# Scan products of a state-space block, two state tiles at a time on parts of the TensorE array

## The reference, cut to what matters

```python
ug = u.reshape(bsz, L, 64, 16)                      # 64 groups of 16 channels, L = 256
bu = einsum('gpc,blgc->blgp', b_bar, ug)            # complex, 64 states a group
h  = scan of h = lam_bar * h + bu along the tokens
y  = einsum('gcp,blgp->blgc', c, h).real + d_skip * ug
```

## Time and profile before

| what | value |
|---|---|
| median of three executions | 2492.57 us |
| profiled execution, its own time | 2492.02 us |
| its span, first to last instruction | 2490.4 us |
| mean granted TensorE clock | 0.964 of full speed |
| TensorE matmuls busy | 2356.1 us, 95% |
| VectorE busy | 1641.5 us, 66% |
| ScalarE busy | 978.7 us, 39% |
| GpSimd busy | 366.8 us, 15% |
| convolution stage with the scan | from 124.2 us to about 654 us |

### The profile page before, as it was taken

The page is one execution under the profiler, slowest core; times in us unless marked ns, Lnnn a source line. Parts: engine busy times, 40 slices in busy tenths (PEclk is TensorE's granted clock), DMA queues, the critical chain, the costliest instruction groups (busy, mean ns, idle before and its releaser), DMA issues.

```text
span 2490.4 us, 52181 instructions
## 1 busy us (share of the span) xinstructions
PE 2356.1 (95%) x20536; PEld 2260.4 (91%) x20536; DVE 1641.5 (66%) x2055; ACT 978.7 (39%) x1210; POOL 366.8 (15%) x214
## 2 busy tenths in 40 slices
PE   5999999999999999699997799899999999999997
PEld 5999999999999999699995677689999999999997
DVE  7688888888545677666798544277565656554444
ACT  4433333333444444433444211244434343434443
POOL 3265555554200000200002000000000000000000
PEclk9999999999999999899997877799999999999999
DMA  5544444445555655255553000035555555555553
GB/s 203 194 162 154 162 163 170 167 160 185 178 185 186 211 174 186 97 185 187 180 194 98 2 2 2 18 125 183 191 185 185 185 185 186 185 171 187 186 185 131
DMA packets 107710, 390.69 MB, mean 157 GB/s; under 512 B 12016, under 2 KB 12144, under 8 KB 107376
## 3 DMA queue, kind: packets, MB, share of 16 engines
q1 hardware_dynamic: 104544, 377.34, 45.8%
q0 software_dynamic: 2656, 11.01, 1.3%
q10 hardware_dynamic: 432, 1.21, 0.1%
HBM read 387.42 MB, written 2.10 MB: 156 GB/s over the span
## 4 chain that ended last, share of the span: by engine, by line
PE 77%; DVE 16%; issue 4%; ACT 1%; DVEq 0%; DMA 0%; ACTq 0%
PE ps_main L1499 22%; PE ps_main L1501 22%; PE ps_main L1500 21%; DVE w_lo L853 5%; PE ps_main L1710 2%; PE ps_aux L1710 1%; PE ps_main L1834 1%; PE ps_main L1833 1%; PE ps_aux L1800 1%; PE ps_aux L1799 1%; PE ps_aux L1499 1%; ACT w_hi L503 1%; DVE m L990 1%; DVE m L991 1%; PE ps_aux L1501 1%
## 5 line engine op out<-in xcount | busy, mean ns | idle before, releaser
L853 DVE TENSOR_TENSOR w_lo<-w_raw,w_hi 128x1024 fp32r<-128x1024 f32 x718 | 943.2, 1328 | 505.2 <-ACT w_hi L503 495.8
L503 ACT ACTIVATE w_hi<-w_raw 128x1024 fp32r<-128x1024 f32 x718 | 749.6, 1047 | 829.6 <-PE ps_main L1501 745.5
L1499 PE MATMUL ps_main<-xs,w_hi 128*128 128x256 f32 x1520 | 430.1, 283 | 10.1 <-DVE w_lo L853 10.1
L1501 PE MATMUL ps_main<-xs,w_lo 128*128 128x256 f32 x1520 | 424.9, 280 | 0.0
L1500 PE MATMUL ps_main<-xs,w_hi 128*128 128x256 f32 x1520 | 424.1, 279 | 0.0
L1499 PE MATMUL ps_main<-x3s,w_hi 128*128 128x256 f32 x1408 | 394.4, 280 | 0.0
L1501 PE MATMUL ps_main<-x3s,w_lo 128*128 128x256 f32 x1408 | 392.8, 279 | 0.0
L1500 PE MATMUL ps_main<-x3s,w_hi 128*128 128x256 f32 x1408 | 392.8, 279 | 0.0
L1499 PEld LDWEIGHTS ps_main<-xs,w_hi 128*128 128x128 f32 x1520 | 284.7, 187 | 18.5 <-DVE w_lo L853 11.5
L1500 PEld LDWEIGHTS ps_main<-xs,w_hi 128*128 128x128 f32 x1520 | 285.3, 188 | 0.4
L1501 PEld LDWEIGHTS ps_main<-xs,w_lo 128*128 128x128 f32 x1520 | 285.4, 188 | 0.0
(11 more groups left out here) (390 smaller groups left out, 4301.4 us busy)
## 6 DMA issues: line engine op xcount, KB each, us to landing
w_raw<-wmain SPq DMA_DIRECT2D x622, 512.0 KB, 3.3
w_raw<-wdown SPq DMA_DIRECT2D x80, 512.0 KB, 3.6
b_stage<-bst POOLq DMA_DIRECT2D x8, 512.0 KB, 5.2
w_raw<-wdown SPq DMA_DIRECT2D x16, 256.0 KB, 2.7
bias<-bias POOLq DMA_DIRECT2D x8, 384.0 KB, 3.3
x_res<-xt POOLq DMA_DIRECT2D x4, 512.0 KB, 7.2
out<-x_res SPq DMA_DIRECT2D x4, 512.0 KB, 2.7
x_res<-xt SPq DMA_DIRECT2D x2, 512.0 KB, 5.9
```

What stands on the lines that cost most here:

```text
L503: nc.scalar.activation(whi[:, s, 0:width], raw[:, s, 0:width], ACT.Copy).then_inc(hi_ready, 1)
L853: V.tensor_tensor(wlo[:, s, 0:width], raw[:, s, 0:width], whi[:, s, 0:width].bitcast(F32), ALU.subtract)\
L1499: nc.tensor.matmul(out, whi[:, s, w], xs_[:, 0, k, :], start=(first and kk == 0), stop=False)
L1501: ins = nc.tensor.matmul(out, wlo[:, s, w], xs_[:, 0, k, :], start=False, stop=(last and kk == kbs - 1))
```

## The change

`b_stage` no longer holds the stored zeros: the 32 rows of each state tile stand on that tile's own 32 partitions, and a matmul of `scan_bu` takes 32 rows of the array (`tile_position=(32 * t, 0)`) with all 128 columns. The load of `b_stage` shrinks from 512 KB to 128 KB a block. The tokens' operand comes from a fixed copy, `u_stage`, that ScalarE makes once a block (`stage_u`): ahead of the loop after `trig(0)`, and in a block at p = 9 after `trig(i + 1)`. TensorE waits for that copy (`u_staged`) before the first products of a block.

`scan_bu` and `scan_y` handle a pair of tiles in one go, in the order part 0 of both tiles, then part 1 of both. The input products stay at p = 0 and 3; the output products go from p = 4, 5, 8, 9 to p = 5 and 9. Each output product still has 128 rows and 32 columns.

```diff
-        bstage = wk("b_stage", 96, [TPB, 2, P])
+        bstage, ustage = wk("b_stage", 96, [2, P]), wk("u_stage", 97, [L])
...
-        SCAN_BU, SCAN_IN, SCAN_Y = (0, 0, 3, 3), (0, 1, 4, 5), (4, 5, 8, 9)
+        SCAN_BU, SCAN_IN, SCAN_Y = (0, 3), (0, 1, 4, 5), (5, 9)
...
                     if p == 9 and not last:
                         trig(i + 1)
+                        act.wait_ge(bu_ready, i * TPB + TPB)
+                        stage_u(i + 1)
...
+            def stage_u(i):
+                nc.scalar.activation(ustage[:, :], slot(ug, i) if not isinstance(i, int) else ug[:, i, :], ACT.Copy)\
+                    .then_inc(u_staged, 1)
+
             trig(0)
+            stage_u(0)
             with act.Fori(0, SB - 1) as i:
...
-            def scan_bu(i, t):
-
-                if t == 0:
+            def scan_bu(i, pair):
+
+                t0 = 2 * pair
+                if pair == 0:
                     pe.wait_ge(b_loaded, i * 16 + 16)
-
-                pe.wait_ge(bu_used, (i * TPB if t < 2 else i * TPB + (t - 1)) + GO)
-                uj = ug[:, bass.ds(i, 1), :].rearrange("p a n -> p (a n)")
-                nc.tensor.matmul(aux[:, t % 2, 0:L], bstage[:, t, 0, :], uj, start=True, stop=True)
-                nc.tensor.matmul(aux[:, t % 2, L:2 * L], bstage[:, t, 1, :], uj, start=True, stop=True)\
-                    .then_inc(bu_ready, 1)
+                    pe.wait_ge(u_staged, i + 1)
+                pe.wait_ge(bu_used, i * TPB + t0 + GO)
+                for part in range(2):
+                    for t in (t0, t0 + 1):
+                        rows = slice(32 * t, 32 * t + 32)
+                        ins = nc.tensor.matmul(aux[:, t % 2, part * L:(part + 1) * L], bstage[rows, part, :], ustage[rows, :],
+                                               start=True, stop=True, tile_position=(32 * t, 0))
+                        if part == 1:
+                            ins.then_inc(bu_ready, 1)
...
-                pe.wait_ge(h_ready, i * TPB + (t + 1) + GO)
-                out = aux[32 * t:32 * t + 32, 2, 0:L]
-                nc.tensor.matmul(out, cstage[:, t, 0, :], hs[:, t % 2, 0, :], start=True, stop=False,
-                                 tile_position=(0, 32 * t))
-                nc.tensor.matmul(out, cstage[:, t, 1, :], hs[:, t % 2, 1, :], start=False, stop=True,
-                                 tile_position=(0, 32 * t)).then_inc(h_used, 1)
+                pe.wait_ge(h_ready, i * TPB + (t0 + 2) + GO)
+                for part in range(2):
+                    for t in (t0, t0 + 1):
+                        ins = nc.tensor.matmul(aux[32 * t:32 * t + 32, 2, 0:L], cstage[:, t, part, :], hs[:, t % 2, part, :],
+                                               start=(part == 0), stop=(part == 1), tile_position=(0, 32 * t))
+                        if part == 1:
+                            ins.then_inc(h_used, 1)
...
-                    for t in range(TPB):
-                        if SCAN_BU[t] == p:
-                            scan_bu(i, t)
-                        if SCAN_Y[t] == p:
-                            scan_y(i, t)
+                    if p in SCAN_BU:
+                        scan_bu(i, SCAN_BU.index(p))
+                    if p in SCAN_Y:
+                        scan_y(i, SCAN_Y.index(p))
```

More of the change, by code:

```diff
@@ L263, in hybrid_kernel @@
         xg_ready, xn_ready, xhi_ready, xs_ready = sem("xg_ready"), sem("xn_ready"), sem("xhi_ready"), sem("xs_ready")
-        ones_ready, c_prime, ga_copied, ga_sig = sem("ones_ready"), sem("c_prime"), sem("ga_copied"), sem("ga_sig")
+        u_staged, ones_ready, c_prime, ga_copied, ga_sig = sem("u_staged"), sem("ones_ready"), sem("c_prime"), sem("ga_copied"), sem("ga_sig")
         ybh_ready, f_ready, mh_ready, x_again = sem("ybh_ready"), sem("f_ready"), sem("mh_ready"), sem("x_again")
@@ L392, in scan_b @@
                 src = bst_dram[0] if isinstance(i, int) else bst_dram[bass.ds(i, 1)].rearrange("a p n -> p (a n)")
-                pool.dma_start(bstage[:, :, :, :], src).then_inc(b_loaded, 16)
+                pool.dma_start(bstage[:, :, :].rearrange("p a n -> p (a n)"), src).then_inc(b_loaded, 16)
             def scan_c(i):
@@ L1558, in scan_y @@
-            def scan_y(i, t):
-                if t == 0:
+                    pe.wait_ge(u_staged, i + 1)
[7 more added lines that the diff above has]
+                            ins.then_inc(bu_ready, 1)
@@ L1561, in scan_y @@
+            def scan_y(i, pair):
+                t0 = 2 * pair
+                if pair == 0:
                     pe.wait_ge(c_staged, i + 1)
                     pe.wait_ge(y_used, i + GO)
-                pe.wait_ge(h_ready, i * TPB + (t + 1) + GO)
-                out = aux[32 * t:32 * t + 32, 2, 0:L]
-                nc.tensor.matmul(out, cstage[:, t, 0, :], hs[:, t % 2, 0, :], start=True, stop=False,
-                                 tile_position=(0, 32 * t))
-                nc.tensor.matmul(out, cstage[:, t, 1, :], hs[:, t % 2, 1, :], start=False, stop=True,
-                                 tile_position=(0, 32 * t)).then_inc(h_used, 1)
+                pe.wait_ge(h_ready, i * TPB + (t0 + 2) + GO)
[5 more added lines that the diff above has]
+                            ins.then_inc(h_used, 1)
@@ L2003, in _layout @@
     arrays["xt"] = np.ascontiguousarray(f["x"][0].T.reshape(KB, P, L).transpose(1, 0, 2))
-    bst = np.zeros((SB, P, TPB, 2, P), np.float32)
+    bst = np.zeros((SB, P, 2, P), np.float32)
     cs = np.zeros((P, 2, STATE_TILES, 32), np.float32)
@@ L2008, in _layout @@
         for g in range(64):
-            j, t, h = g // 8, g % 8 // 2, g % 2
-            bst[j, (g % 8) * 16:(g % 8) * 16 + 16, t, r, h * 64:h * 64 + 64] = b[g].T
+            j, h = g // 8, g % 2
+            bst[j, (g % 8) * 16:(g % 8) * 16 + 16, r, h * 64:h * 64 + 64] = b[g].T
             cs[h * 64:h * 64 + 64, r, g // 2, h * 16:h * 16 + 16] = c[g].T
-    arrays["bst"] = bst.reshape(SB, P, TPB * 2 * P)
+    arrays["bst"] = bst.reshape(SB, P, 2 * P)
     arrays["cs"] = cs
```

## The result

The changed kernel takes 2510.78 us (median of eight executions; the kernel before 2492.47 in eight), a ratio of 1.0062 with a 95% interval of 1.0043 to 1.0082. By the ratio it is slower by some 15 us, by the two medians by 18. The forecast was 2495.4, "no change", with a range of 2485 to 2510: the median lies just above its upper end, and the ratio times the median before (2508) just inside it.

A forecast was written before the change was run, and what follows sets the result against it. VectorE's w_lo chain paces each block up to unit 15, PE the rest. First block +3.39, crossings +0.5, last block gaining 2.84, clock +1.7: +2.8 on 2492.02, 2494.8; with 0.55 for the median 2495.4 us, range 2485 to 2510.

The forecast's parts named there:

- Block split into A and B: A, end of unit 0 to unit 15's w_lo, VectorE paces; B, to the next unit 0's end, PE paces, savings count.
- Input pair, 1.27 us: scan_bu pair on PE: 1.27 instead of 1.85 us, 0.58 saved, 0.48 where PE comes straight from dense work.
- Output pair, 1.18 us saved: scan_y pair on PE: two tiles side by side take 1.18 instead of 2.36 us.
- Wait for `u_stage`: PE before each block's first products: waits 1.8 us, 3.9 in the first block; blocks stay at 66.5 us.
- Last block: No w_lo to wait for, so it gains 0.48 + 2 x 1.18 = 2.84 us.
- The clock: One half-clock stretch, 1.7 us, behind the first block's wait; none added for gaps in the seven blocks.
- the sum of +2.8: Whole kernel against the profiled 2492.02 us: net +1.1 from the blocks, 1.7 for the clock, giving 2494.8.
- the clock falls in every block: Rival: half-clock stretch behind unit 15's gap, 1.7 us in each of seven blocks, 12 us, 2507; chance 0.12.
- the two slower rivals: Tiles do not run side by side, 2509 us, chance 0.10; clock falls in every block, 2507, chance 0.12.

The follow-up runs named there:

- The pair with tripled output products: Kernel of the early copy with one pair's output products issued three times, at p = 5 or at p = 9; ratios 0.9956 and 0.9998.
- the plain wait: Kernel before with only the copied operand, u_stage made behind trig and PE's wait for it, products as before; ratio 1.0078.
- the kernel with the output products alone: Kernel before with the changed kernel's scan_y, output products in pairs at p = 5 and 9; ratio 0.9961.
- the kernel of the early copy: Changed kernel with u_stage made early: in the zb stage for the first block, at p = 6 for the others; ratio 0.9953.
- The kernel with the filled gap: Changed kernel with fifteen dense matmuls on TensorE ahead of its wait for u_stage in each block; ratio 1.0022.

## Why the prediction came out as it did, step by step

- **Block split into A and B**: right. Savings in A went into the waits for `w_lo` (10.1 us in 7 before, 19.8 in 14 after, at units 11 and 15). The pair with tripled output products shows it from the other side.
- **Input pair, 1.27 us**: right. Its eight passes take 1.13 us from first start to last end, and with them a block is 0.57 to 0.67 shorter than with the plain wait (67.80 against 68.37 to 68.47, all without a half-clock stretch), where 0.58 was forecast. Row tiles of 32 rows run side by side as those of 64 did.
- **Output pair, 1.18 us saved**: right, 1.15 by the kernel with the output products alone.
- **Wait for `u_stage`**: right in place, with gaps of 1.78 us and 3.93 in the first block, 1.8 and 3.9 forecast. A block without a half-clock stretch is 66.6 us, not 66.48: the copy takes 0.40 us, not the 0.36 read off `gate_a`, and PE starts 0.13 behind it, not 0.05. Over seven crossings that is about 1 us.
- **Last block**: right. From its first input products to the gb stage it was forecast 3.42 shorter (2.84, and the 0.58 that I had counted with the crossing); it is 1.83 shorter (62.87 against 64.70) with a half-clock stretch that cost some 1.5 in it, and 3.37 shorter in the kernel of the early copy, which has none.
- **The clock**: this is the step that failed. "In the seven blocks the gaps become about 1.7 us at `stage_u` and 1.9 at unit 15 ... I add none." The term for the clock was put at one stretch, 1.7 us. All eight gaps at `stage_u` were followed by a half-clock stretch, each worth 1.5 to 1.6 us: 12.3 us instead of 1.7. With it and the 1 us above, the sum of +2.8 becomes +14.4, against 14.7 measured for the stage. The rival "the clock falls in every block" had the right size, and 0.12 of the chance; it had the place wrong, at unit 15's stall, where the changed kernel has none and other kernels three in all. I compared gaps by length alone (1.45 kept, 2.19 fell). The kernel with the filled gap shows that the idle time is needed; the early copy, that the light products without it are harmless. Why the gaps of 1.78 us fell here and not in the kernel with the wait alone stays open: lighter work behind them and another place in time are both possible, and gaps of 1.9 us with dense work behind them fell too.
- **The range**: that the result lies at its edge is owed to its width, taken for the two slower rivals, and not to the sum. A time slower by over 0.5%, as it came, had been given 0.16.

The Trainium skill, TensorE: Matmul & The Clock Gate, section on HAM oscillation, warns of bursts with idle time between; the waits in its own case are about 3 to 5 us. The trace agrees that idle time can be followed by half clock, and shows it behind shorter gaps than those: 1.8 us, in a stream that is otherwise dense.

## What to carry to other kernels

Work taken off the busiest engine is won only in the stretch where that engine sets the pace: find the stall, and ask which part of the loop lies ahead of it. An operand copied for the sake of a faster form needs its own place in the queue of the engine that copies it; here, exchanging two lines turned 0.6% slower into 0.7% faster. Before adding a wait on TensorE where it sets the pace, count more than the wait: a gap of 1.8 us cost up to 1.6 us more here by the clock, and whether it did could not be told from its length alone. And when an engine's steps are slow beside another's, moving them to where nobody waits can be enough; here it took the kernel of the early copy from 0.5% faster to 1.3%, with the same work.

## What the runs showed of the hardware that I had not expected

- A gap of 1.78 us was followed by half clock in 0 of 7 crossings with full 128-row products behind it, in 8 of 8 blocks (the first with a gap of 3.93), 6 of 7 and 3 of 7 with products of 32 rows side by side, and in 0 of 7 when dense matmuls filled it. The same gap and products gave both outcomes within one execution. With dense work behind, stalls of 1.70 to 1.72 us were followed by it in 0 of 54 cases and stalls of 1.91 to 1.93 us in 3 of 4.
- A half-clock stretch of 3.4 us cost 1.52 us where PE sets the pace (69.32 against 67.80 for a block).
- Two tiles of 32 rows, and two of 32 columns, did run side by side in fp32 as the wider ones of the trace before: eight passes in 1.13 and in 1.06 us, where eight full ones take 1.7 (a step of 0.215 for each).
